# Filling the short convolution's input earlier, and dealing TensorE's k-tiles between the attention steps anew

## The reference

```python
h = rms_norm(x, norm_g)
z = h @ w_in        # split into x_rnn, g_rnn, sc_b, sc_c, x_sc, g_sc, c_q, c_kv, k_rope, g_att, gates
y_rnn = (rg_lru(x_rnn, ...) * silu(g_rnn)) @ rg_out
y_sc  = (sc_b * causal_depthwise_conv(sc_c * x_sc, sc_conv_w) * silu(g_sc)) @ sc_out
y_att = (mla(c_q, c_kv, k_rope, ...) * silu(g_att)) @ mla_out      # 8 heads, causal softmax
merged = gates[0] * y_rnn + gates[1] * y_sc + gates[2] * y_att
return x + merged @ w_out
```

## Time and profile before

| | |
|---|---|
| time, median of 3 runs | 1672.87 us (1672.76 to 1673.4) |
| the profiled execution: its time | 1674.52 us |
| its span in the trace | 1672.7 us |
| PE busy (matmuls) | 1663.2 us, 99% |
| DVE busy | 1157.2 us, 69% |
| ACT busy | 600.9 us, 36% |
| POOL busy | 1257.1 us, 75% |
| DMA, mean | 104 GB/s |

### The profile page before, as it was taken

One profiled execution on the slowest core, in us unless ns is written; L12 is line 12 of the kernel. 1 busy time (PEld: TensorE's weight loads), 2 busy tenths in 40 slices (PEclk: granted clock), 3 DMA queues, 4 the chain that ended last, 5 costly groups with the idle time before them and its releaser, 6 DMA issues.

```text
span 1672.7 us, 32259 instructions
## 1 busy us (share of the span) xinstructions
PE 1663.2 (99%) x11912; PEld 1566.6 (94%) x11912; DVE 1157.2 (69%) x1622; ACT 600.9 (36%) x1073; POOL 1257.1 (75%) x1334
## 2 busy tenths in 40 slices
PE   9999999999999999999999999999999999999999
PEld 8999999999999999999998888888888888999887
DVE  7966758485677778776349657484847887778751
ACT  5523333242344344432135233332323434444320
POOL 7774848385899869897866748483868997899983
PEclk9999999999999999999999999999999999999999
DMA  4432223222333243432532313232323334333333
GB/s 164 142 100 64 94 62 93 68 82 93 104 107 101 101 141 115 125 116 76 167 119 77 112 60 97 63 92 68 93 86 106 101 113 141 114 127 127 113 101 116
DMA packets 52746, 173.19 MB, mean 104 GB/s; under 512 B 6544, under 2 KB 7952, under 8 KB 52624
## 3 DMA queue, kind: packets, MB, share of 16 engines
q1 hardware_dynamic: 44352, 153.04, 28.9%
q10 hardware_dynamic: 8320, 19.17, 3.3%
HBM read 156.53 MB, written 15.14 MB: 103 GB/s over the span
## 4 chain that ended last, share of the span: by engine, by line
PE 88%; DVE 7%; issue 2%; ACT 1%; DMA 0%; ACTq 0%; DVEq 0%; SPq 0%; POOL 0%; POOLq 0%
PE slots L656 65%; PE slots L940 13%; PE slots L721 3%; PE slots L755 3%; PE slots L739 1%; PE slots L828 1%; DVE early L1591 1%; DVE early L1606 1%; DVE qr_hi_and_lo L1418 1%; DVE kr_lo L1418 1%; DVE kn_lo L1418 1%; PE slots L690 1%; PE slots L706 0%; DMA residual_or_merged<-xt 0%; DVE early L1613 0%
## 5 line engine op out<-in xcount | busy, mean ns | idle before, releaser
L525 POOL TENSOR_TENSOR w_lo<-w_raw,w_hi 128x256 fp32r<-128x256 f32 x828 | 737.7, 920 | 17.3
L520 POOL TENSOR_SCALAR w_hi<-w_raw 128x1024 fp32r<-128x1024 f32 x207 | 251.7, 1216 | 206.4 <-PE slots L656 191.7
L656 PE MATMUL slots<-h_hi,w_hi 128*128 128x264 f32 (+1 forms) x1584 | 379.7, 307 | 0.9 <-DVE sc_pad L1719 0.9
L656 PE MATMUL slots<-h_lo,w_hi 128*128 128x264 f32 (+1 forms) x1584 | 374.2, 304 | 0.0
L656 PE MATMUL slots<-h_hi,w_lo 128*128 128x264 f32 (+1 forms) x1584 | 373.9, 303 | 0.0
L656 PEld LDWEIGHTS slots<-h_hi,w_hi 128*128 128x128 f32 x1584 | 255.0, 188 | 13.7 <-issue 2.0
L656 PEld LDWEIGHTS slots<-h_hi,w_lo 128*128 128x128 f32 x1584 | 254.2, 188 | 11.6
L656 PEld LDWEIGHTS slots<-h_lo,w_hi 128*128 128x128 f32 x1584 | 254.4, 188 | 10.7
L595 POOL TENSOR_TENSOR w_lo<-w_raw,w_hi 128x256 fp32r<-128x256 f32 x132 | 126.0, 986 | 43.5 <-ACT w_hi L1329 43.5
L656 PE MATMUL slots<-branch_hi,w_hi 128*128 128x264 f32 (+1 forms) x552 | 143.4, 319 | 2.0 <-DVE branch_lo L1431 2.0
L656 PE MATMUL slots<-branch_lo,w_hi 128*128 128x264 f32 (+1 forms) x552 | 141.5, 315 | 0.0
(11 more groups left out here) (279 smaller groups left out, 3796.0 us busy)
## 6 DMA issues: line engine op xcount, KB each, us to landing
w_raw<-w_units SPq DMA_DIRECT2D x251, 512.0 KB, 3.6
stream<-sc_acc ACTq DMA_DIRECT2D x16, 264.0 KB, 2.1
stream<-h_blend ACTq DMA_DIRECT2D x8, 528.0 KB, 2.7
h_mixes<-stream SPq DMA_DIRECT2D x8, 528.0 KB, 4.6
sc_back<-stream SPq DMA_DIRECT2D x8, 528.0 KB, 3.7
x_old<-stream SPq DMA_DIRECT2D x16, 264.0 KB, 4.6
stream<-residual_or_merged ACTq DMA_DIRECT2D x16, 264.0 KB, 2.9
ab_raw<-w_units SPq DMA_DIRECT2D x8, 512.0 KB, 4.3
```

The costliest lines, as they stand in the source:

```text
L520: pool.tensor_scalar(hi, raw, 1.0, 1.0, ALU.mult, ALU.mult).then_inc(sem("hi_part"), 1)
L525: op = pool.tensor_tensor(lo[:, cols], raw[:, cols], hi[:, cols].bitcast(F32), ALU.subtract)
L656: mm = pe.matmul(out[:, a_, 0:t1 - t0], w(k), x(k)[:, t0:t1], start=(n == 0), stop=(n == 3 * ks - 1))
```

## The change

Two things. On DVE `sc_input(0)`, the product of x0 and c0, moves from behind the reciprocal of `q_ms` (just ahead of step 0) to ahead of the two `qr_lo` subtractions, the lower parts of the rotary queries. And the lists FILLS have other numbers of k-tiles: in both layers 17 instead of 16 in the second entry, ahead of the first scores; in layer 0 also 5 instead of 4 in step 1, 6 instead of 7 in step 9 and 5 instead of 6 behind the last step; in layer 1 also 7 instead of 8 behind the last step. The sum stays 80 k-tiles in each pair. PE's instructions keep their kind, number and order among the fills; only the places between them at which scores, transposes and `attend` stand are shifted.

```diff
--- before.py
+++ after.py
@@ -80,7 +80,7 @@
 
 
 FILL = ("c0", "x0", "g0", "b0", "ga0", "c1", "x1", "g1", "b1", "ga1")
-FILLS = ((8, 16, 4, 4, 4, 5, 5, 2, 6, 6, 7, 7, 6), (8, 16, 4, 4, 8, 6, 2, 8, 8, 8, 8))
+FILLS = ((8, 17, 4, 5, 4, 5, 5, 2, 6, 6, 7, 6, 5), (8, 17, 4, 4, 8, 6, 2, 8, 8, 8, 7))
 PLAIN = 1
 BUFFERS = {"MR": (0, 1, 2, 0, 1, 2), "MS": (0, 1, 2, 3)}
 PAIR_LIST = [("MR", i, n, j) for i in range(4) for n, j in (("a", 0), ("g", 3))] + [("MS", i, "g", 0) for i in range(4)]
@@ -1639,6 +1639,14 @@
                         if h == 0:
                             dve.wait_ge(*at("kr_blank", l, 0, 2))
                         lo_part(kr_lo[rows, h, :], ct[4 + h][rows], kr_hi[rows, h, :], "krp_lo")
+                    def sc_input(s):
+
+                        dve.wait_ge(*ready("ATT", l, p, f"x{s}"))
+                        dve.wait_ge(*was_read("ATT", l, p, f"c{s}"))
+                        dve.tensor_tensor(halves(s_pad[:, SCONV - 1:]), slot(slot_of("ATT", f"x{s}")),
+                                          halves(s_c[:]), ALU.mult).then_inc(freed("ATT", f"x{s}"), 1)
+
+                    sc_input(0)
                     for h in range(2):
                         rows = slice(ROPE * h, ROPE * h + ROPE)
                         other = slice(ROPE * (1 - h), ROPE * (1 - h) + ROPE)
@@ -1712,13 +1720,6 @@
                         dve.wait_ge(*at("att_hi", l, p, h + 1))
                         lo_part(kept(l, tile(y_lo, p * 2 + h)), kept(l, spare[h][:]), kept(l, tile(y_hi, p * 2 + h)), "att_lo")
 
-                    def sc_input(s):
-
-                        dve.wait_ge(*ready("ATT", l, p, f"x{s}"))
-                        dve.wait_ge(*was_read("ATT", l, p, f"c{s}"))
-                        dve.tensor_tensor(halves(s_pad[:, SCONV - 1:]), slot(slot_of("ATT", f"x{s}")),
-                                          halves(s_c[:]), ALU.mult).then_inc(freed("ATT", f"x{s}"), 1)
-
                     def sc_conv(s, m):
 
                         c = p * 2 + s
@@ -1753,7 +1754,6 @@
                         dve.scalar_tensor_tensor(kept(l, s_acc[:]), kept(l, s_acc[:]), 0.5, kept(l, s_g[:]), ALU.mult,
                                                  ALU.mult).then_inc(sem("sc_full"), 1)
 
-                    sc_input(0)
                     for n in range(2 * STEPS[l]):
                         row_bias(n)
                         scale_rows(n)
```

## The result

| | before | after |
|---|---|---|
| time, median of 6 runs each | 1672.9 us (1672.56 to 1674.34) | 1718.73 us (1715.12 to 1730.72) |
| the profiled execution: its time | 1674.52 us | 1718.02 us |
| its span | 1672.7 us | 1716.2 us |

The ratio after/before is 1.0281, 95% interval 1.0267 to 1.0295: 2.8% slower. The forecast was slower by 30.1 us with a range up to 1711 us, so the direction was right and the time lies above the range. All ratios here are of fast executions; the only slow one was one of e1's twelve, with 2945.57 us at a granted clock of 0.753.

The account below looks back on a forecast made before the run. TensorE, busy 1663.2 of 1672.7 us, was taken to bound the kernel. Net waits of 5.6 + 5.4 (ga0) and 10.8 + 8.3 (x1) = 30.1 us on the median 1672.87 gave 1703.0 us, range 1695 to 1711.

Parts of the forecast that it names:

- The counting of the k-tiles: Summed FILLS lists: k-tile 32 (ga0) falls inside step 1, k-tile 48 (x1) inside attend(0)'s step; each waits in 8 pairs.
- Rival (a): Slots for ga0 and x1 come free sooner, the waits do not bite, only 2.9 us gains stay: 1670.0 us; chance 0.04.
- rival (b): Only the wait at k-tile 48 (x1) bites: 16.2 us more, 1689 us; chance 0.06.
- Part 1: Earlier sc_input(0) on VectorE: its 0.71 us is hidden by the extra k-tile; b0 gains 0.34 us a pair in layer 1.
- the cover of 0.07 us: Layer 1, ahead of the first scores: time to spare between qr_lo's release at 1019.50 and TensorE's arrival at 1019.57.
- Rival (c): sc_input(0) is not covered and the scores come late as well: 5.7 us more, 1709 us; chance 0.06.
- the forecast sum: Net waits at ga0 5.6 and 5.4 us, at x1 10.8 and 8.3 us (layers 0 and 1): 30.1 us.
- the forecast's reading, that passes are short where GpSimd rests: Convolution passes on VectorE before sc_gate(0): kept at 1.0 us each beside busy GpSimd; shortest passes would give 1697 us.
- part 4: The other moves: borders 40, 56, 64, 72, attend(1), load queue and GpSimd; all costed at nothing, hidden by fills.
- rival (d): Clock falls to 1.2 GHz behind the eight longest waits, another 3.0 us each: 1727 us; chance 0.04.
- TensorE's busy time stays near 1663: Expected sign over the whole program: TensorE's busy time, 1663.2 us before, stays near 1663 us after the change.
- the forecast's own sign of being wrong: The prediction is wrong if the 16 waits are missing, scores wait for qr_lo, or a slice shows a lower clock.

Follow-up runs that it names:

- e1: The kernel before with only sc_input(0) moved earlier as in the change, FILLS lists as before; 1674.39 against 1674.31 us, ratio 1.0001.
- e2: The changed kernel with k-tile 48 put back behind the step of sc_copy(1), only k-tile 32 early; 1688.81 against 1674.31 us for the kernel before.
- e3: The kernel before with lists that move only k-tile 48 (x1) into the step with attend(0); 1713.66 against 1674.31 us.
- e5: The kernel before with k-tile 48 in attend(0)'s step, but more c1 k-tiles ahead of x1 there; 1683.51 against 1673.39 us.
- e10: The changed kernel with sc_copy(1) and sc_gate(0) earlier, second convolution pass later, layer 1 list 7, 1; 1681.88 against 1674.41 us for the kernel before.
- e6: The changed kernel with 24 (layer 1: 20) unused matmuls added ahead of x1's first k-tile; 1705.73 against 1673.39 us for the kernel before.
- e4: The kernel before with the change's new lists, sc_input(0) in its old place; 1735.36 against 1674.31 us.
- e9: The changed kernel with sc_copy(1) ahead of soften(n) on ScalarE and layer 1's list 7, 1 instead of 6, 2; 1691.18 against 1674.41 us for the kernel before.

## Why the prediction was right and wrong

**The counting of the k-tiles held.** Both borders bite where the lists said, 16 times, with the releasers named; e2 and e3 show them one at a time. Rival (a), that they don't bite, and rival (b), that only k-tile 48 does, are out.

**Part 1 held.** VectorE in the same pair, after the change, to compare with the earlier trace rows:

```profile
280.49 0.71 DVE L1646 TENSOR_TENSOR sc_pad<-slots,sc_c 128x528 f32<-128x528 f32 x1
281.23 2.56 DVE L1418 TENSOR_TENSOR qr_hi_and_lo<-early,qr_hi_and_lo 64x528 fp32r<-64x528 f32 x2
```

`qr_lo` ends at 283.79, and the scores start at 284.74. In layer 1 the cover of 0.07 us, counted, was enough: no wait for `qr_lo` stands in the list. Rival (c) is out.

**The waits came out at the forecast sum, by luck: two errors of opposite sign.** ga0 in layer 0 waits until 292.56 where 291.15 + 0.24 = 291.39 was possible: 1.17 us, not 1.80; with the transposes of step 0 0.18 us late, and 0.39 gained, net 0.96 instead of 1.41. In layer 1 it is 1.33 - 0.34 = 0.99 instead of 1.35. Times 4 and 4 that is 7.8 us instead of 11.0. x1 waits from 309.41 to 312.52, 3.11 instead of 2.70 us, and in layer 1 2.61 instead of 2.07: 22.9 us instead of 19.1. The sum is 30.7 against 30.1 us.

Both errors come mainly from the lengths of VectorE instructions, which I kept at those of before. VectorE and GpSimd of the changed kernel at the two places:

```profile
285.76 1.04 DVE L1676 SCALAR_TENSOR_TENSOR r_bias<-r_max,q_sc 106x1 f32<-106x1 f32 x1
...
287.60 0.78 DVE L1687 TENSOR_SCALAR residual_or_merged<-residual_or_merged,r_inv 106x106 f32<-106x106 f32 x1
288.30 0.48 DVE L1729 TENSOR_SCALAR sc_acc<-sc_pad,channel_params 128x528 f32<-128x528 f32 x1
...
291.49 0.33 DVE L1687 TENSOR_SCALAR residual_or_merged<-residual_or_merged,r_inv 106x212 f32<-106x212 f32 x1
291.73 0.70 DVE L1740 SCALAR_TENSOR_TENSOR sc_gate<-sc_gate,slots 128x528 f32<-128x528 f32 x1
...
310.76 0.57 DVE L1676 SCALAR_TENSOR_TENSOR r_bias<-r_max,q_sc 106x1 f32<-106x1 f32 x1
```

```profile
285.75 1.04 POOL L520 TENSOR_SCALAR w_hi<-w_raw 128x1024 fp32r<-128x1024 f32 x1
...
310.60 0.72 POOL L525 TENSOR_TENSOR w_lo<-w_raw,w_hi 128x256 fp32r<-128x256 f32 x1
```

At ga0's place the first pass took 0.48 instead of 1.00 us and the scaling of step 1 0.33 instead of 0.88, while `r_bias` and the first scaling took more. On balance the chain from the scores of step 0 to the end of `sc_gate(0)` takes 7.69 us instead of 8.08, and TensorE reaches the border 0.24 us later: together the 0.63 us between 1.80 and 1.17. The pass was short although GpSimd's split ran beside it (x4 from 286.87 to 290.53), so the forecast's reading, that passes are short where GpSimd rests, does not cover it. At x1's, `r_bias` took 0.57 instead of 0.16 us, which is the whole 0.41 that layer 0's wait is longer; in layer 1 it took 0.69 instead of 0.16, the 0.54 there. The step of the forecast that failed here is in part 4, "the load queue and GpSimd follow TensorE", costed at nothing: GpSimd's split moved beside this chain. Before, GpSimd stood still from 294.12 to 298.34, with `r_bias` at 297.82; now it is at work from 308.79 on, with `r_bias` at 310.76. That the split lengthens `r_bias` is read from 144 instructions (last section), not from an experiment. It came to 4 x 0.41 + 4 x 0.54 = 3.8 us, the difference of 22.9 and 19.1.

**What made the forecast wrong is the clock, rival (d), to which I gave 0.04.** The step that failed is "TensorE's busy time stays near 1663": the sum has no term for the clock. Of the 14.2 us more, 1.4 to 2.1 come with the waits alone (e2, e5, e10, without a lower clock), so 12.1 to 12.8 us are the clock; e6 gives 12 by another way. The 30.7 us of waits leave 12.8 of the 43.5, of which 0.8 are `branch_lo`'s at the start.

The six executions of the changed kernel give it a third way. Their granted clock over the span runs from 0.993 (1715.12 us) down to 0.982 (1730.72 us). One minus the clock, times the span, is the time at full speed that was not granted, 12.0 to 31.1 us, and the time grows by 0.81 us with each microsecond of it (my estimate, by a line through the six points). At full clock that line is at 1705.6 us, near the forecast's 1703.0 and e6's 1705.73; for the profiled execution, at 0.991, it gives 12.5 us. So most of the spread of the changed kernel's times is also the clock: how much of it is lost varies from one execution to the next.

Rival (d) was put at eight times 3.0 us; it came behind six of eight, at about 2.1 us each, and 1718.73 lies between the forecast's 1703 and its 1727. The fault was the weight; the forecast's own sign of being wrong, a slice with a lower clock, came up in one slice. The earlier trace rows showed a steady upper clock in a kernel whose longest wait was 1.6 us, at the very start of the program, and 1.0 us behind it, and I took "no row has a wait of 2.7 us" as evidence against a fall behind such a wait. It was none: the forecast itself made the first such waits. The range ended at 1711 and left this case out.

The Trainium skill (TensorE: Matmul & The Clock Gate, Why this matters for your kernels) warns that idle gaps between bursts of matmuls bring the clock back. The runs here agree in kind: it fell behind waits of 2.0 to 3.0 us, and without the gap at x1 (e6) it did not fall there. They do not agree in length: the page speaks of gaps at least as long as the longest here, so the forecast's "by that rule (d) would be the outcome" read more into it than it says, and the clock fell behind shorter ones.

## What to carry to other kernels

When a schedule puts a border of a buffer into the step that produces its release, sum the chain from that step's first instruction to the release; it is paid in full each time. When the forecast puts TensorE into idle stretches longer than any in the profile of before, that profile says nothing about the clock behind them: give a fall of the clock a real chance and let the range reach it. Read the busy time of the engine whose instructions are unchanged, and book span = waits + busy; where busy grew by more than the 1.4 to 2.1 us that the waits alone brought here, look at the clock in windows of a few microseconds, even if the page's digits stay at nine.

## What the runs showed of the hardware

- Over all kernels here, the granted clock was lower behind 23 of 31 waits of TensorE of 2.0 to 3.0 us: 20 of the 24 x1 waits of the changed kernel, e3 and e4, 1 of 4 of 2.4 us in e4, and 2 of 3 of 2.0 us (e6 and e9, not e2). It was not lower behind any wait of 0.9 to 1.2 us. Behind the start of the program no run has a wait between 1.2 and 2.0 us, so where between the two it begins is open. The fall came between 1.3 us before and 1.4 us after the wait's end, and the clock stayed at 1.2 GHz for 3.4 to 10.2 us, with TensorE at work again. Why it stays up behind some long waits is open; the same place fell in one kernel and not in another.
- A 106x1 VectorE instruction, 0.16 us alone, can take 1.04 us: `r_bias` at 285.76 ends at 286.80, when GpSimd's instruction ends (285.75 + 1.04), and at 310.76 it ends at 311.33, with GpSimd's at 310.60 + 0.72 = 311.32. Over the 144 `r_bias` instructions of the kernel before and the changed one, the 48 beside which no GpSimd instruction ran took 0.16 us; the 71 that took 0.20 to 1.04 us all ended within 0.03 us behind the end of a GpSimd instruction; beside the other 25, also 0.16 us long, one ran for a part of the time only. The Trainium skill (SBUF — State Buffer, Who interferes with whom) says that a VectorE instruction with two inputs in SBUF contends with a GpSimd instruction that reads SBUF, and that the pair of ports that they share is an exclusive lock; `r_bias` has two such inputs, and the traces agree with it. No run here took GpSimd's work away, so the cause rests on this coincidence of the ends and not on an experiment.
